# A gated delta layer: triangular systems solved in two halves of 32 columns, and a projection moved from the front stage to among the chunks

## The reference

```python
qkv, z, b_logit, a_logit = split(h @ w_in)            # h is 512 x 1024
qkv = silu(causal_depthwise_conv(qkv, conv_w))         # 4 taps
a_mat = where(strict, einsum('id,jd->ij', kb, k) * decay, 0)   # 64 x 64 per head and chunk
ia = a_mat + eye(64)
u = triangular_solve(ia, vb)                           # unit lower triangular
w = triangular_solve(ia, kb * exp(g))
def step(s, (q_c, k_c, u_c, w_c, qk_c, sd_c)):         # the 8 chunks in turn
    v_new = u_c - w_c @ s
    o_c = q_c @ s + qk_c @ v_new
    s = s * sd_c + k_c.T @ v_new
o = rms_norm(o, norm_w) * silu(z)                      # z: the gate, 16 heads x 128
```

## Time and profile before

| | |
|---|---|
| median of 3 runs | 3339.64 us (3339.34 to 3340.68) |
| the profiled execution, its own time | 3338.5 us |
| its span in the trace | 3336.5 us |
| TensorE busy in the span | 2891.9 us, 87% |
| VectorE busy | 1964.7 us, 59% |
| ScalarE busy | 1188.1 us, 36% |
| GpSimd busy | 675.3 us, 20% |
| mean granted TensorE clock | 0.921 of full speed |

### The profile page before, as it was taken

How to read it: one execution, slowest core, us unless ns; L and a number is a source line. 1 busy time by engine, 2 the same in 40 slices (tenths; PEclk the granted TensorE clock), 3 DMA queues, 4 the chain that set the end, 5 groups by cost and what they waited for, 6 DMA issues and landing times. The chain is left out here.

```text
span 3336.5 us, 40537 instructions
## 1 busy us (share of the span) xinstructions
PE 2891.9 (87%) x15338; PEld 2537.4 (76%) x15338; DVE 1964.7 (59%) x3367; ACT 1188.1 (36%) x2033; POOL 675.3 (20%) x378
## 2 busy tenths in 40 slices
PE   5787669978998999998999999698857768799987
PEld 4787438867888998898888887587746668688877
DVE  4324442336997988666888887347984543344433
ACT  3323442223334776432333332574213431322221
POOL 0002110002332333364333231243320110000000
PEclk8898779989999999999999999799986779899999
DMA  2102012124335888899999997384325422222222
GB/s 108 66 10 78 2 39 101 63 101 160 117 126 176 296 304 305 316 358 366 355 361 354 361 358 286 110 240 156 124 86 165 145 95 86 101 90 98 101 89 83
DMA packets 226657, 578.72 MB, mean 173 GB/s; under 512 B 35184, under 2 KB 127216, under 8 KB 194384
## 3 DMA queue, kind: packets, MB, share of 16 engines
q1 hardware_dynamic: 187776, 434.44, 38.6%
q0 software_dynamic: 36864, 134.23, 10.3%
q10 hardware_dynamic: 1872, 8.13, 0.7%
HBM read 488.49 MB, written 88.21 MB: 173 GB/s over the span
## 5 line engine op out<-in xcount | busy, mean ns | idle before, releaser
L40 PE MATMUL pe_ps<-hh,pe_uh 128*128 128x384 f32 x1024 | 351.8, 344 | 24.5 <-issue 18.3
L41 PE MATMUL pe_ps<-hl,pe_uh 128*128 128x384 f32 x1024 | 346.2, 338 | 0.0
L42 PE MATMUL pe_ps<-hh,pe_ul 128*128 128x384 f32 x1024 | 346.2, 338 | 0.0
L40 PE MATMUL pe_ps<-pe_vh,pe_whi 128*128 128x512 f32 x768 | 299.8, 390 | 4.6 <-DVE pe_vl L1498 4.6
L41 PE MATMUL pe_ps<-pe_vl,pe_whi 128*128 128x512 f32 x768 | 299.7, 390 | 0.0
L42 PE MATMUL pe_ps<-pe_vh,pe_wlo 128*128 128x512 f32 x768 | 299.6, 390 | 0.0
L1325 POOL DMA_INDIRECT pe_gu<-in_u_rows,pe_urow x128 | 200.7, 1568 | 314.4 <-DVE pe_gu L1459 289.1
L1333 POOL DMA_INDIRECT pe_gv<-in_v_w,pe_vrow x128 | 157.2, 1228 | 333.5 <-DVE pe_acc L1468 319.8
L40 PEld LDWEIGHTS pe_ps<-hh,pe_uh 128*128 128x128 f32 x1024 | 195.6, 191 | 26.9 <-issue 26.4
L40 PE MATMUL sc_ps<-hh,sc_wh 128*128 128x512 f32 x512 | 199.9, 390 | 12.8 <-DVE sc_wl L2542 12.8
L1459 DVE SCALAR_TENSOR_TENSOR pe_gu<-pe_gu,pe_xs 128x1024 f32<-128x1024 f32 x128 | 155.1, 1220 | 94.0 <-DMA pe_gu<-in_u_rows,pe_urow 93.8
(11 more groups left out here) (457 smaller groups left out, 7255.3 us busy)
## 6 DMA issues: line engine op xcount, KB each, us to landing
xu<-in_u_w SPq DMA_DIRECT2D x64, 1024.0 KB
pe_v_raw<-in_v_w SPq DMA_DIRECT2D x64, 1024.0 KB, 8.5
sc_raw<-in_sc_w SPq DMA_DIRECT2D x32, 1024.0 KB, 4.9
hidden_scratch<-pe_hs SPq DMA_DIRECT2D x64, 384.0 KB
gate_scratch<-pe_stage SPq DMA_DIRECT2D x24, 1024.0 KB, 11.3
pe_hw<-hidden_scratch SPq DMA_DIRECT2D x64, 384.0 KB
pe_gate<-gate_scratch SPq DMA_DIRECT2D x64, 384.0 KB
gf_raw<-in_gdn_w SPq DMA_DIRECT2D x24, 1024.0 KB, 6.7
```

The costliest lines, as they stand in the source:

```text
L40: pe.matmul(out, lh, rh, start=start, stop=False)
L41: pe.matmul(out, lh, rl, start=False, stop=False)
L42: return pe.matmul(out, ll, rh, start=False, stop=stop)
```

## The change

It does four things.
- The substitution runs on the two diagonal blocks of 32 columns of each system at once: 31 steps of two instructions over 2 x (j+1) x (31-j) elements. The halves stand in `ut`; a turned copy of the first, the second, the untouched corner of `at` and a block of zeros are put into one tile that goes to DRAM as `rc_scratch` (2 MB more).
- The corner of the inverse is computed in the back stage by two float32 TensorE products of four 128 x 128 blocks each, for 16 bursts `n` of four chunks of a lane: `corner(n)` on TensorE (L2538), `corner(n)` on ScalarE (the two instructions to `m1`), `merge(n)` on TensorE (L2544), `merge(n)` on VectorE (two copies into `ub`). Two bursts are done ahead, the others in chunks 0, 1, 2 and 5 of a pair (`due`).
- The eight gate iterations leave the front stage. The same 384 matmuls are issued in the back stage three at a time (`next(ahead)`), four times in a chunk, with weight tiles of 512 KB: `load_z(f)` on SP, `high(f)` and `gate(f)` on ScalarE, `low(f)` on GpSimd, in chunks of odd number. The gates no longer pass through DRAM.
- In the front stage the low parts of tiles 10 to 15 are computed by VectorE (`low`) and not by GpSimd.

```diff
-        room = [0] * (KH + 1) + [4] + [6] * (KH - 1) + [11] * (KH - 2) + [0]
+        work = [(j + 1) * (H - 1 - j) + H for j in range(H - 1)]
+        OWN = KH + 2
+        room = [0] * (KH + 1) + [3] + [6] * 4 + [0] * (KH - 6)
...
                 for it in range(NB):
...
+                    if it == KH + 6:
+                        sp.wait_ge(elim, 2 * (H - 1))
+                        sp.dma_start(ud_dram.rearrange("a h i c t -> (a h i) (c t)"), utf).then_inc(u_out, 16)
+                        sp.wait_ge(turned_u, 1)
+                        sp.wait_ge(kept_u, 1)
+                        sp.wait_ge(cleared, 1)
+                        sp.dma_start(rc_dram.rearrange("a h i c t -> (a h i) (c t)"), flat(at)).then_inc(u_out, 16)
...
                 def eliminate(j):
-                    m, n, done = j + 1, C - 1 - j, 2 * j
+                    m, n, done = j + 1, H - 1 - j, 2 * j
...
+                def low(n):
+                    dve.wait_ge(w_hi, n + 1)
+                    dve.tensor_tensor(wl[n % 2][:], raw[n % 2][:], wh[n % 2][:].bitcast(F32), ALU.subtract).then_inc(w_lov, 1)
...
+                def load_z(f):
+                    if f >= 2:
+                        sp.wait_ge(z_lo, f - 1)
+                    sp.dma_start(raw[f % 2][:], w_dram[f // 2, 2][:, :, f % 2 * P:(f % 2 + 1) * P]).then_inc(z_in[f % 2], 16)
...
                 for g in range(LAST):
+                    c, i = g // NCH, g % NCH
                     if g + 3 < LAST:
                         load(0, g + 3)
                         load(1, g + 3)
+                    if i % 2 and g // 2 + 2 < 2 * KH:
+                        load_z(g // 2 + 2)
...
+                def high(f):
+                    act.wait_ge(z_in[f % 2], 16 * (f // 2) + 16)
+                    if f >= 2:
+                        act.wait_ge(z_mm, f - 1)
+                    act.activation(wh[f % 2][:], raw[f % 2][:], ACT.Copy).then_inc(z_hi, 1)
...
                 for g in range(LAST):
                     c, i = g // NCH, g % NCH
+                    if due(c, i) is not None:
+                        corner(due(c, i))
                     carried(0, g)
                     fresh(0, g)
                     carried(1, g)
                     fresh(1, g)
                     if g and g % B == 0:
                         square(1, g - 1)
+                    if i % 2:
+                        gate(g // 2)
+                        if g // 2 + 2 < 2 * KH:
+                            high(g // 2 + 2)
...
+                def merge(n):
+                    l, u = n % 2, n // 2 % 3
+                    dve.wait_ge(ub_in[u][l], 32 * (n // 6) + 32)
+                    dve.wait_ge(m2_mm, n + 1)
...
                 for g in range(LAST):
                     c, i = g // NCH, g % NCH
                     rest(0, g)
+                    if due(c, i) is not None:
+                        merge(due(c, i))
                     if g:
                         state(1, g - 1)
                     rest(1, g)
```

More of the change, by code:

```diff
@@ L1814, in _ @@
                 differ(0)
[L1815 to L1819, removed]
+                for it in range(1, KH):
+                    low(it + 2)
+                    differ(it)
+                pool.wait_ge(elim, 2 * (H - 1))
+                pool.memset(at[:, H:C, H:C], 0.0).then_inc(cleared, 1)
             @block.scalar
@@ L2027, in _ @@
                             eliminate(j)
+                    if it == KH + 5:
+                        dve.wait_ge(elim, 2 * (H - 1))
+                        dve.tensor_copy(at[:, 0:H, 0:H], ut[:, 0:H, 0:H].rearrange("p c s -> p s c")).then_inc(turned_u, 1)
+                values(KH - 1)
             @block.tensor
@@ L2451, in turn @@
                     pe.wait_ge(scaled, 2 * c + l + 1)
-                    if 4 * c + 2 * l + half >= 2:
-                        pe.wait_ge(joined, 4 * c + 2 * l + half - 1)
+                    pe.wait_ge(merged, min(4 * (c + 1) + 5 + l, NM))
+                    if 4 * c + 2 * l + half:
+                        pe.wait_ge(joined, 4 * c + 2 * l + half)
                     for j in range(B):
-                        last = pe.transpose(ps[:, BT[half], j * P:(j + 1) * P], og[c % 2][l][:, half * B + j, :], ident[:])
+                        last = pe.transpose(ps[:, BT, j * P:(j + 1) * P], og[c % 2][l][:, half * B + j, :], ident[:])
                     last.then_inc(turned, 1)
+                for n in range(2):
+                    corner(n, 0)
+                    next(ahead)
+                    next(ahead)
+                    merge(n)
                 for g in range(LAST):
                     c, i = g // NCH, g % NCH
+                    n = due(c, i)
+                    if n is not None:
+                        corner(n, 4 * max(c - 1, 0) + (2 if c and i == 5 else 0))
                     carry(0, g)
+                    next(ahead, None)
                     if g:
```

217 lines of the change are left out of this document (150 added, 67 removed).

## The result

| | before | after |
|---|---|---|
| median of the runs | 3339.49 us (3335.82 to 3340.68, 4 runs) | 3393.45 us (3384.74 to 3394.51, 4 runs) |
| the profiled execution and its span | 3338.5, 3336.5 us | 3392.6, 3390.8 us |
| back stage begins (GpSimd's first clear) | 2505.08 us | 2388.33 us |
| first `fresh` to last `within` ("the loop" below) | 2510.9 to 2700.7, 189.8 us | 2416.2 to 2750.1, 333.9 us |

The changed kernel is slower: the ratio of the times is 1.0158, 95% interval 1.0139 to 1.0176. The front stage won 116.75 us. The back stage gave back 22.1 us ahead of the loop (27.9 us from its first clear to the first `fresh`, where it was 5.8), 144.1 in the loop and 3.3 in the last pair's scaling and joining. The remaining 1.5 us of the 54.3 between the spans lie outside the two stages.

What follows compares the result with a forecast made beforehand. VectorE's substitution set the front stage's end; in the chunk loop no engine was full and half a chunk was a chain. Back +157.5 and front -115 on 3338.5, with 1.1 for the median, gave 3382 us; range 3312 to 3436.

Steps and rivals of the forecast that it cites:

- Front stage: Up to the back stage: shorter substitution without GpSimd blocks, gate iterations gone; gain 115 us (105 to 121).
- The drain: End of the front stage: 5 MB go out from 2371.5 in some 16 us, plus 2 us for the barrier.
- TensorE's work: Back stage: old loop's rows, corners, gates and changes between matmul kinds take 223 us, 217 in the loop, 6 ahead.
- The merge wait: Chunks 1, 2 and 5: `merge` ahead of `state` on VectorE idles TensorE 1.2 us, ten times, 12 us.
- ScalarE's wait: Odd chunks: `high` waits for a weight tile requested late, holding up TensorE; 70 us over 14 tiles (50 to 98).
- The clock: Chunk loop: the 14 gaps lower TensorE's clock and slow the work behind them; 25 us (5 to 78).
- Loop: Chunk loop: 217 work, 12 merge wait, 9 `scale` and `join`, 70 ScalarE's wait, 25 clock; 333 us.
- Ahead of the loop: Back stage before the chunk loop: clears, first corner load and two corners take 18.5 us (14 to 21).
- Tail: End of the back stage: one bank for all turns costs 2 us.
- ScalarE hardly waits: Rival for the chunk loop: tiles land early and the clock holds; 3292 to 3327, say 3310 us; chance 0.18.
- The low clock stays: Rival for the chunk loop: clock at 0.70, 217 becomes 310; +53 us, 3435 us; chance 0.14.
- GpSimd did not block `scale`: Rival, back stage: GpSimd's low parts block the eight `scale`, up to 19 us more, 3401; chance 0.05 as main error.

Runs made afterwards that it cites:

- e4: Changed kernel with the low parts of value tiles 10 to 15 back on GpSimd; 3395.7 us, ratio 1.0173 to the kernel before.
- e8: Changed kernel with three edits together: weight tile early (e1), state before merge (e3), corner tiles first (e5); 3269.3 us, ratio 0.9803 to the kernel before.
- e7: e1 with only the high x high product of each gate product, 128 matmuls in place of 384; 3287.0 us, ratio 0.9843 to the kernel before.
- e11: e8 with only the high x high product of each gate product, 256 of 384 wide matmuls left out; 3258.4 us, ratio 0.9764 to the kernel before.
- e3: Changed kernel with VectorE taking state(1, g - 1) before merge(n) instead of after it; 3369.0 us, ratio 1.0103 to the kernel before.
- e1: Changed kernel with SP asking for the gates' weight tile a chunk earlier, ahead of load(0, g + 3); 3295.8 us, ratio 0.9874 to the kernel before.
- e5: Changed kernel with corner tiles cleared and asked for earlier, ahead of the chunk loop; 3383.2 us, ratio 1.0135 to the kernel before.
- e9: e8 with gates back in eight front-stage iterations, through DRAM, and substitution in iterations 9 to 19; 3324.4 us, ratio 0.9965 to the kernel before.

## Why the prediction was right

The forecast was 3382 us with 0.77 for slower; 3393 came, for the reason given. By its own steps:

- **Front stage**, 115 us: 116.75. The substitution took 32.6 us of rows and some 2.5 of the gaps between them for 34.9. Iteration 10 began at 2304.5 (2303.7), the last value ended at 2379.1 (2380). The low parts took 2.28 us each, and no instruction was blocked. The Trainium skill (SBUF — State Buffer, Who interferes with whom) says that two such instructions shut each other out; e4 agrees, with 4.91 us for 0.62 until GpSimd's subtract ended.
- **The drain**: the two transfers of 2 MB were asked for at 2370.55 and 2371.24 (2371.5), and the back stage began 17.8 us after the first; I had 16 for the transfers and 2 for the barrier. No row shows the barrier by itself.
- **TensorE's work**, 217 in the loop: e8's 222 us at full clock, of which 206 busy, show it was about right: with the 9 of `scale` and `join` I had 226 without the two new waits. As a price for the gates it misleads (e7, e11): they lie over waits of the chain.
- **The merge wait**, 12 us: 13.3 in ten waits. What it costs the loop is more, 23 us in e3 and 21 from e1 to e8, and this the sum did not have.
- **ScalarE's wait**, 70 us in 14 tiles: 70.9 in 14 waits of TensorE. The tile landed in 4.4 us (4.0 taken). e1 changes only the place of the request, and the waits went.
- **The clock**, 25 us: 26 of busy time less in e1, which had the same work. The rule that I set beside it (the Trainium skill, TensorE: Matmul & The Clock Gate, HAM oscillation — how this bites in real kernels) has every gap cost; the trace agrees for twelve of the 14, the window at 0.53 among them, and not for the gaps of 3.15 and 3.37 us, which kept 1.00.
- **Loop**, 333: 333.9. That these agree to 1 us is in part luck. By the experiments the parts are 222.4 for e8's loop (226 forecast), 90.5 for ScalarE's wait with its clock (95) and 21 for the merge wait (12): the last was too low by as much as the first two were too high. `scale` and `join` were not tried apart.
- **Ahead of the loop**, 18.5 us in 14 to 21: 27.9. This step failed. I followed the first two corners, and they took what I wrote: the second's copies end at 2407.03, 18.7 us after the first clear. But the loop's first `fresh` stands behind the third corner product, which I left out. Its tile was asked for at 2405.22, and TensorE waits 6.0 us for it, 5.3 of them behind those copies; e5 gives this back. From 2412.37, when the tile is there, to that `fresh` at 2416.19 are another 3.8 us.
- **Tail**, 2: 3.3.

With these the back stage is +169.5 instead of +157.5, and the spans differ by 54.3 us where I had 42.5. Of the rivals, "ScalarE hardly waits" gave 3310; e1, in which it does not, is at 3296. "The low clock stays" is not what happened, 0.85 against 0.70. GpSimd did not block `scale`: all eight take 1.21 to 1.23 us.

## What to carry to other kernels

When a change puts a new load into an in-order queue, look at what the request ahead of it waits for, and at what stands behind the instruction that will wait for the data. Here a request behind the waiting `pk` loads of its chunk cost 90 us over 14 tiles, more than the 64 that the whole move of the gates saves, and ahead of these two loads it costs 5. Work that fills a dependent chain's waits costs less than its length: 87 us of products cost 13 (e8 against e9), if what feeds them, which stands in the chain's own queues, never makes these queues wait.

## What the runs showed of the hardware that was not expected

A short wait right behind a long gap costs more than its own time. In the three places where a wait of 1.4 us followed a gap of 5.9 to 7.7 us, some 5 us of rows at the low clock came on top of 4.1 us of waiting (e3). Seven waits of 1.3 to 1.4 us elsewhere, in full clock, left it full. In e1, three waits of 2.7 to 2.9 us have a clock of 0.57 to 0.76 in the 6 to 7 us behind them, and in e8, without them, it is 1.00 throughout. Nor is the length of a gap alone what decides: 3.04, 3.11 and 3.17 us were followed by a low clock, 3.15 and 3.37 us were not.

The loop without wide products sits at 0.81 with 161 of 208 us busy; with them it is at 1.00 with 206 of 222. I had expected that leaving out 58 us of products would give back some 44 us (e7). It gave 18.5: the clock and the chain kept 40.
